# A two-layer hybrid-attention trunk: blocks 3 and 2, and 1 and 0, share one score step in three of its four branches

## What is computed

```python
h = split_cols(x @ w_in)
out_a = causal_dense_attention(qa, ka, va, key_valid, HEAD_DIM ** -0.5, decay)
out_b = mla_attention(h['b_cq'], h['b_ckv'], h['b_kr'], g_q, g_kv, w_uq, w_ukv, pos, key_valid)
out_c = dsa_sparse_attention(..., key_valid, rel_bias[:, :DSA_HEADS], top_k)
out_d = sliding_window_sink_attention(..., key_valid, rel_bias[:, DSA_HEADS:], sinks)
mixed = jnp.concatenate([
    out_a * jax.nn.silu(h['a_g']), out_b * jax.nn.silu(h['b_g']),
    out_c * jax.nn.silu(h['c_g']), out_d * jax.nn.silu(h['d_g'])], axis=-1)
return layer_norm(ALPHA * x + mixed @ w_out, ln_g, ln_b)
```

## Time and profile before

| | value |
|---|---|
| median of three runs | 2945.43 us (2944.47 to 2949.46) |
| the profiled execution's own time | 2943.56 us |
| span of the profiled execution | 2941.6 us |
| mean granted TensorE clock | 0.994 of full speed |
| TensorE busy | 2854.4 us, 97% of the span |
| VectorE, ScalarE, GpSimd busy | 55%, 36%, 22% |

### The profile page before, as it was taken

One profiled execution on the slowest core, in us unless ns is written; L12 is line 12 of the kernel. 1 busy time (PEld: TensorE's weight loads), 2 busy tenths in 40 slices (PEclk: granted clock), 3 DMA queues, 4 the chain that ended last, 5 costly groups with the idle time before them and its releaser, 6 DMA issues. The chain is left out here.

```text
span 2941.6 us, 39580 instructions
## 1 busy us (share of the span) xinstructions
PE 2854.4 (97%) x13638; PEld 1675.1 (57%) x13638; DVE 1621.2 (55%) x4361; ACT 1059.6 (36%) x3085; POOL 642.6 (22%) x1336
## 2 busy tenths in 40 slices
PE   7999999999999999999999999999999999999998
PEld 5446666555566666644544466665555666665443
DVE  5337888767776433322333388886767764323232
ACT  3334444343455345500012334443334544445000
POOL 1002333111122244500000022331112222444000
PEclk9999999999999999999999999999999999999999
DMA  6201111111110121042120011111011101201421
GB/s 225 66 8 47 44 44 33 38 33 45 37 32 19 33 99 33 26 149 79 58 91 31 10 45 44 44 33 45 28 43 37 33 17 33 106 28 30 155 86 43
DMA packets 90908, 156.88 MB, mean 53 GB/s; under 512 B 11296, under 2 KB 67248, under 8 KB 88920
## 3 DMA queue, kind: packets, MB, share of 16 engines
q1 hardware_dynamic: 90712, 154.36, 16.4%
HBM read 120.13 MB, written 32.08 MB: 52 GB/s over the span
## 5 line engine op out<-in xcount | busy, mean ns | idle before, releaser
L1160 PE MATMUL ps_s<-xT,w_ring 128*128 128x348 f32 (+4 forms) x3616 | 1122.4, 464 | 12.6 <-DVE gate L1617 5.0
L1160 PEld LDWEIGHTS ps_s<-xT,w_ring 128*128 128x128 f32 x3616 | 673.3, 191 | 396.4 <-issue 102.6
L1412 ACT ACTIVATE arena<-ps_t 16x32 f32<-16x32 f32 (+3 forms) x1048 | 367.2, 373 | 239.9 <-PE ps_t L1230 225.7
L1399 ACT ACTIVATE arena<-arena,small 128x1040 f32<-128x1040 f32 (+8 forms) x544 | 372.0, 684 | 132.4 <-DVE small L1679 131.6
L1442 DVE MAX8 small<-score 128x8 f32<-128x1040 f32 (+6 forms) x448 | 376.3, 840 | 10.5
L1444 DVE MATCH_REPLACE8 score<-small,score 128x1040 f32<-128x1040 f32 (+6 forms) x448 | 370.0, 826 | 0.0
L1230 PE MATMUL ps_t<-ident,arena 128*128 128x128 f32 (+1 forms) x2016 | 300.5, 278 | 13.0 <-ACT arena L1412 12.9
L1791 POOL TENSOR_SCALAR strips<-arena,small 128x16 f32<-128x16 f32 x384 | 107.1, 279 | 902.2 <-DVE small L1691 902.2
L1203 PE MATMUL ps_s<-feat 64*128 64x272 f32 (+12 forms) x1680 | 295.6, 454 | 3.3 <-ACT arena L1315 3.2
L1230 PEld LDWEIGHTS ps_t<-ident,arena 128*128 128x128 f32 (+1 forms) x2016 | 224.2, 140 | 116.6 <-issue 67.0
L1794 POOL TENSOR_SCALAR arena<-arena,small 128x1024 f32<-128x1024 f32 (+7 forms) x384 | 286.2, 745 | 0.0
(11 more groups left out here) (177 smaller groups left out, 2504.8 us busy)
## 6 DMA issues: line engine op xcount, KB each, us to landing
w_ring<-in_w_feat SPq DMA_DIRECT2D x78, 512.0 KB, 3.5
mixed<-mixg SPq DMA_DIRECT2D x128, 128.0 KB, 1.7
feat<-mixed SPq DMA_DIRECT2D x16, 1024.0 KB, 6.7
resid<-score SPq DMA_DIRECT2D x16, 512.0 KB, 3.2
score<-resid SPq DMA_DIRECT2D x16, 512.0 KB, 7.6
arena<-in_w_out SPq DMA_DIRECT2D x4, 1536.0 KB, 8.0
cT<-falls SPq DMA_DIRECT2D x8, 520.0 KB, 4.8
feat<-falls SPq DMA_DIRECT2D x8, 520.0 KB, 5.2
```

The costliest lines, as they stand in the source:

```text
L1160: mm = pe.matmul(ps_s[:, bank, 0:w], w_ring[:, wt % 2, k, :], xT[:, k, c0:c0 + w], start=(k == 0), stop=(k == KT - 1))
L1399: nc.scalar.activation(p, p, ACT.Exp, scale=-1.0, bias=nm[:, e:e + 1], accum_out=psums[0:M, st % 4, e:e + 1]).then_inc(S["exp_done"], 1)
L1412: a = nc.scalar.activation(dst, src, ACT.Copy)
```

## The change

It has these parts.

1. **Shared score steps.** In A, B and C the pair walks rounds of blocks, `[[8],[7],[6],[5],[4],[3,2],[1,0]]`; D keeps single blocks. One `qk` item holds the scores of both blocks of a round, and VectorE takes both maxima there. `rec` becomes a list: the reciprocals of blocks 3 and 2 stand behind the maxima of 1 and 0, those of 1 and 0 behind the maxima of the next pair's block 8. The `pv` of blocks 6 and 5 moves behind the scores of 1 and 0, that of 4 and 3 behind the next pair's first scores. In B, the scores of blocks 3 and 2 are no longer cut in two.
2. **C's fill.** G and the next pair's Q are written in half chunks (4 matmuls) at steps 0, 0, 1, 1, 2, 3, 4, 5, 6, 7, 7, 8; in p3 G's halves stand at 0, 0, 1, 1, 2, 3.
3. **B's fill.** From p1 on, the next pair's query products stand at steps 5, 6, 7 and no longer at 3, 4, 5.
4. **D's fill.** `LATENT_STEPS` gives TB and `ct` by a table: in p2 TB of 8 and 6 and `ct` of 5 at step 6, TB of 7 and `ct` of 8 at step 7, `ct` of 6 at step 8; in p3 `ct` of 7 moves from step 0 to step 1. The rotation's step 2 moves from step 6 to step 7.
5. **Top-256 search.** D runs 5 of its operations in steps 0 to 2 of p0 to p2, and in p3 4, 4, 4, 4, 3, 2, 2, 2, 3.
6. **Prologue.** Blocks are normalised in place; block 8 (the first) by VectorE, the others by ScalarE (one activation with scale and bias), for which GpSimd runs two more operations a block. A first activation loads ScalarE's table at the start, 20 transposes of nothing run on TensorE before the first block, and two small VectorE operations move behind the nine blocks.

```diff
+TOP_RATE = {..., "D": [5, 5, 5, 4, 4, 4, 4, 4, 4], "D3": [4, 4, 4, 4, 3, 2, 2, 2, 3], ...}
+LATENT_STEPS = [[([0], []), ([1], [0]), ([2], [1])], [([3], [2]), ([4], [3]), ([5], [4])],
+                [([8, 6], [5]), ([7], [8]), ([], [6])]]
...
+def rounds_of(br):
+    return [[i] for i in ORDER] if br == "D" else [[8], [7], [6], [5], [4], [3, 2], [1, 0]]
...
-        products = even(n, 2 if n >= 272 else 1)
+        products = even(n, 2 if i > 3 else 1)
...
+    def halves(self, l, what, **kw):
+        out, wt = [], self.open()
+        for c in (2, 1, 0) if what == "G" else range(3):
+            begun = {}
+            out.append(lambda c=c, begun=begun: begun.update(self.chunk(l, wt, what, c, k1=KT // 2, **kw)))
+            out.append(lambda begun=begun: self.add(**dict(begun, k0=KT // 2, k1=KT)))
+        return out
...
-                put(0, lambda: self.latent(l, NB - 2))
+                fill[1].insert(0, lambda: self.latent(l, NB - 2))
...
-                for idx, step in ((5, 0), (6, 1), (6, 2), (7, "dup")):
+                for idx, step in ((5, 0), (6, 1), (7, 2), (7, "dup")):
...
-                for idx, work in zip((3, 4, 5), self.q_latent(l, p + 1)):
+                for idx, work in zip((3, 4, 5) if p == 0 else (5, 6, 7), self.q_latent(l, p + 1)):
...
-            for idx, work in zip((3, 4, 5), self.tile(l, "Q", br="C", p=p + 1)):
+            rest = self.halves(l, "G", br=br, p=p) + self.halves(l, "Q", br="C", p=p + 1)
+            for idx, work in zip((0, 0, 1, 1, 2, 3, 4, 5, 6, 7, 7, 8), rest):
...
-        for idx, i in enumerate(ORDER):
+        for blocks in rounds_of(br):
+            steps = [self.step(l, br, p, i, hu) for i in blocks]
+            if steps:
+                self.add("qk", l=l, br=br, p=p, idx=steps[0]["idx"], hu=hu, steps=steps, ready=steps[0]["ready"])
+                self.normalise()
+                self.values()
+            self.pending += steps
+            for s in steps:
+                old = self.pending.pop(0) if len(self.pending) > LAG else None
+                if old and old["i"] == 0:
+                    self.values()
+                self.probabilities(old, 0)
+                self.add("exp", e=0, **s)
+                self.gated()
+                self.add("top", l=l, count=top_rate(br, p)[s["idx"]])
...
+            self.rec_next += steps
```

More of the change, by code:

```diff
@@ L414, in pair @@
         put = lambda idx, work: fill.setdefault(idx, []).append(work)
[L415 removed]
+        for idx, work in enumerate(self.tile(l, "G", br=br, p=p) if br != "C" else []):
             put(idx, work)
@@ L427, in pair @@
                     put(idx, work)
[L428 to L434, removed]
+                for idx, (blocks, turned) in zip((6, 7, 8), LATENT_STEPS[p]):
+                    for b in blocks:
+                        if b == NB - 1:
+                            put(idx, lambda: self.token_block(l, "TB", NB - 1, bank=self.free_bank()))
+                        else:
+                            put(idx, lambda b=b: self.token_block(l, "TB", b))
+                    for b in turned:
+                        put(idx, lambda b=b: self.latent(l, b))
                 if p == NP - 2:
@@ new lines, in pair, with step @@
+        if l == DEPTH - 1:
+            self.empty_step(l, br, p, early, fill.get(NB - 1, []))
+        return None
+    def step(self, l, br, p, i, hu):
+        st = self.take("st")
+        chunks, products = [], []
+        some = score_products(br, i)
+        for nth, ((c0, w), pieces) in enumerate(some):
+            banks = self.slot_for(len(some), nth, P_BANK)
+            last = self.n["chunk"] + len(pieces) - 1
+            waits = self.banks(banks, ("max_done", 2 * (last + 1)))
+            if O_BANK in banks:
+                waits = latest(waits + [("o_free", self.n["pv"])])
+            products.append(dict(c0=c0, w=w, banks=banks, pieces=len(pieces), waits=waits))
+            chunks += [dict(c0=a, w=b, banks=banks, at=a - c0, g=self.take("chunk"), full=2 * (last + 1))
+                       for a, b in pieces]
+        row, at = row_of(br, i)
+        owner = self.row_owner[row]
+        n = min(keys_of(i), 2 * BLK) if br == "D" else keys_of(i)
+        return dict(l=l, br=br, p=p, i=i, st=st, idx=NB - 1 - i, n=n, M=rows_of(i), chunks=chunks, products=products,
+                    row=row, at=ROW_AT[row] + at, ready=sorted(self.ready.items()) if i == NB - 1 else [],
+                    rwaits=latest([owner] if owner else []), a=(i + 1) // 2, hu=hu,
+                    ds=self.take("ds") if br == "D" else None, tri=self.take("tri") if br == "A" else None,
+                    nb=self.take("nb") if br == "C" else None)
@@ L1084, in _ @@
             pe.wait_ge(S["id_ld"], 16)
+            for _ in range(20):
+                pe.transpose(ps_t[:, 0, 0:BLK], ident[:], ident[:])
             for it in items:
@@ L1527, in _ @@
+                    if ln >= NB + 2:
+                        dve.wait_ge(x_st[r], 16 * len([n for n in range(ln - 1) if n % 2 == r]))
                         if it["xprev"]:
```

287 lines of the change are left out of this document (149 added, 138 removed).

## The result

The changed kernel takes 2956.83 us in the median of 7 runs (2954.79 to 2959.97), the kernel before 2945.43 us in as many. The ratio is 1.0040 with a 95% interval of 1.0030 to 1.0049: slower by 11.4 us. The forecast said no change, with 2946.0 us; the time lies in the stated range of 2925 to 2962 us, but outside the forecast's own 2938 to 2953. The profiled execution's span is 2952.9 us, 11.3 above that of before.

A forecast was written before the change was run, and what follows sets the result against it. The prediction took TensorE's fixed order as the bound. Its terms summed to +0.3 us on the profiled 2943.56 us; with the median's 1.87 us that is 2945.7, stated as 2946.0, no change, range 2925 to 2962 us.

The forecast's parts named there:

- Prologue, -5.5: Blocks before the index stage: no store wait before the norm, and shorter steps a block, -5.5 us.
- Shared scores, -2.4: A and C: two score sets side by side share part of a fixed cost, 24 meetings by 0.1, -2.4 us.
- A's tails, +6: A: block 3's late reciprocals make TensorE wait 1.3 us in p0 and p1, 0.2 in p2 and p3; +6 us.
- B's tails, +5: B: block 3's reciprocals move one step back, waits of 0.6 us a pair in the mean of eight, +5 us.
- D's fifth operation, +2.9: D's steps 0 to 2: the fifth search operation, with A's last reciprocals, costs +2.9 us for both layers.
- D's latents, +5.6: D: the 3.38 us wait stays, block 7's latent in p3 waits 4.3 us in place of 1.56; +5.6 us.
- End of D, -4.5: End of D: search operations and a rotation step leave, the 3.05 us wait falls to about 0.8; -4.5 us.
- The clock, -1.8: Half-speed stretches: +4 behind D's p3 wait, -3.4 behind the second layer's end of D, -2.4 in C; together -1.8 us.
- C's tails, -5: C's pair ends: half chunks let ScalarE's copies catch up, -1 for six pairs, +0.5 in each p3; -5 us.
- the 0.4 that the forecast set as its sign: C's p0 to p2: the changed profile would show no wait over 0.4 us.
- The second rival: A's and B's tails: each of sixteen pairs loses a whole VectorE operation more, +13 us, 2959 us; chance 0.18.
- The first rival: A's and B's tails are covered, their 6 and 5 us go, perhaps a clock dip too: 2931 us; chance 0.32.

The follow-up runs named there:

- best2_cold: best2 without the 20 transposes of nothing ahead of the prologue: 2919.31 us, ratio 0.9913 to the kernel before.
- ab_single: The changed kernel with A and B walking single blocks again, C keeping shared score steps: 2947.28 us, ratio 1.0006 to the kernel before.
- best1: The changed kernel with A, B single, B's query products and rotation's step 2 back, latent scaled before search, D's fifth search operation in steps 3 to 5: 2921.81 us.
- rot_back: The changed kernel with the rotation's step 2 back at step 6 of D's p3: 2951.28 us, ratio 1.0020 to the kernel before.
- c_single: The changed kernel with C walking single blocks again, half chunks kept: 2954.22 us, ratio 1.0032 to the kernel before.
- best2: best1 with C in single blocks too, so no shared score step is left: 2918.23 us, ratio 0.9914 to the kernel before.

## Why the prediction was right or wrong

*Prologue, -5.5: right.* -5.05, by the steps named; ScalarE's norm takes 1.24 us, inside the bounds. This execution has a half-speed stretch in its prologue; the six traces without one (run best2_cold, above) gain 6.2 to 6.5.

*Shared scores, -2.4: wrong in sign.* The step that failed is that two sets of scores side by side only share a start. They also leave two sets of transposes side by side, and these wait 0.4 us for a copy. In pairs without any wait for GpSimd (A's p2 and p3) the change is +0.13 to +0.25 us a pair, in C +0.1 to +0.25 against single blocks. The shared start itself came about as forecast: where the wait adds 0.4 us and the pair grows by 0.13 to 0.25, some 0.15 to 0.27 us a pair were saved.

*A's tails, +6: the mechanism right, the size too large.* VectorE is 1.8 us late where 1.5 was the estimate, and the wait in p1 is 1.14 where 1.3 was. But the second layer's waits are 0.75 and 0.90, and p2 and p3 have none: 3.8 us in all. A's pairs lost 5.6 us, near the 4.8 that the forecast makes with A's half of the shared scores, because the two misses cancel. That is luck.

*B's tails, +5: half of the mechanism.* B lost 9.0 us. Block 3's transposes wait 3.3 of them, in p0 and p1, as forecast and below the 5. The step that failed is that "only the 2.74 us `pv` moves with them": the forecast used this `pv` as cover for block 3 and didn't ask what it had covered before. That was block 4, whose 3.3 us of slack went, and which waits 4.1 us. B's moved query products have no term in the forecast at all; with single blocks they cost 1.8 us. Some 1.6 us of the 9.0 is a half-speed stretch at the start of B in the second layer, which went with the transfer's wait.

*D's fifth operation, +2.9: right* (1.42 and 1.60 us in p0, with A single, by ab_single against best1).

*D's latents, +5.6: right in place and size.* 3.39 us and 4.03 (4.16 in the second layer), where 3.38 and 4.3 were expected: the second wait grew by 2.5 and 2.6 us.

*End of D, -4.5: wrong.* "The wait falls to about 0.8 us" came true (0.82 and 0.97), but what is late next was not asked. Moving the rotation's step 2 one step on also moved the transfer of its result, which takes a median of 3.5 us from issue to landing in the kernel before (this row is of its DMA view: tile, issuer, count, size, time):

```profile
qr_two<-feat SPq DMA_DIRECT2D x2, 260.0 KB, 3.5
```

B's first scores wait 2.60 and 2.26 us for it. With the copy's wait that is 3.42 and 3.23 us, where 3.05 and 3.16 stood before: +0.4 instead of -4.5. This is the largest miss. Besides, D's new fill brings the waits of 0.65 and 0.64 us on ScalarE in p2 and p3, 2.6 us in both layers, for which the forecast has no term.

*The clock, -1.8: partly right.* The window behind the first layer's 3.38 us wait in the kernel before (columns as in rows 1):

```profile
721.00:726.00 5.00, 5.00 (x16) 3.07 (x16) 3.25 (x11) 2.59 (x11) 0.52 (x2) 0.50 0.52 197
```

Windows of the changed kernel, the first behind the same wait:

```profile
721.50:726.00 4.50, 4.50 (x23) 2.89 (x22) 3.25 (x11) 2.88 (x11) 0.53 (x2) 1.00 0.57 216
733.40:736.80 3.40, 3.24 (x8) 2.25 (x9) 0.10 (x1) 0.89 (x3) 0.00 (x0) 0.50 0.00 0
...
2204.50:2211.30 6.80, 4.46 (x10) 3.05 (x11) 2.22 (x6) 0.88 (x3) 0.00 (x0) 0.50 0.03 8
2252.30:2255.70 3.40, 3.40 (x16) 1.34 (x14) 0.00 (x0) 0.00 (x0) 0.00 (x0) 0.50 0.00 0
1590.10:1593.50 3.40, 3.40 (x8) 1.21 (x5) 2.94 (x14) 1.62 (x4) 0.00 (x0) 0.50 0.00 0
```

The lower level followed the 4 us wait in both layers, as said, and C's two stretches went. But it did not follow each of the two waits: behind the first layer's 3.39 us the granted clock reads 1.00, where the kernel before and the run rot_back, with the same wait, have 0.50. Behind the end of D in the second layer it did not go but moved behind the new wait, and one stretch came in the second layer's index stage. In the forecast's sum, -3.4 for a stretch with 6.25 busy us is a little much: half of them is 3.1.

*C's tails, -5: right in size, and the half chunks are the cause*, as c_single shows. Waits of 0.41 and 0.52 us stay in p1 and p2, just above the 0.4 that the forecast set as its sign.

The parts missed by +0.45 (prologue), +0.8 (A with its share of the scores' -2.4), +4.0 (B), +3.9 (D with its clock) and +1.9 us (C with its clock): 11 us between the +0.3 of the sum and the +11.3 of the spans. D's +3.9 hides a larger miss. Up to B's first scores TensorE waits 10.4 us longer than before in the two layers, where the forecast's terms without the clock make 4.0, and less half speed in D (13.7 us of it in place of 20.5) took some of that back. The second rival's time (2959) was near, but not its mechanism: GpSimd's 13.3 us are close to the 11 that the forecast itself gave A's and B's tails, and 7.1 of them stand where it put them, before block 3. The first rival fell.

## What to carry to other kernels

Putting two like steps together on the engine that bounds the kernel also moves what fed it: ask which result now has one step less to arrive, what the work that moved had covered until then, and what stood between two uses of the same buffer. When work on a side engine is moved later to free the path, follow its output too, through its transfer, to whoever reads it first. A scaling that the bound engine waits for belongs ahead of filler on its engine: that order alone was worth 15 us here, more than the change's whole effect.

## What the runs showed of the hardware

Equal waits did not always bring the same clock. In best1 a wait of 0.77 us in B's p1 was followed by half speed, in best2 the same wait with the same work was not:

```profile
876.09 0.33 PE L1297 MATMUL ps_t<-ident,arena 128*128 128x128 f32 x1 [0.77 <-ACT arena L1490]
...
877.20 3.46 PE L1314 MATMUL ps_o<-arena 128*64 128x256 f32 x20 [0.38 <-ACT arena L1490]
```

```profile
874.52 0.33 PE L1297 MATMUL ps_t<-ident,arena 128*128 128x128 f32 x1 [0.77 <-ACT arena L1490]
...
875.63 1.88 PE L1314 MATMUL ps_o<-arena 128*64 128x256 f32 x20 [0.37 <-ACT arena L1490]
```

The same 20 matmuls took 3.46 and 1.88 us, and this p1 58.01 and 56.43. Most pairs with the same work have lengths that repeat to 0.02 us between kernels; one into which such a stretch of 3.4 us falls is about 1.6 us longer. The Trainium skill, "TensorE: Matmul & The Clock Gate", Part 1, says that one kernel shows different numbers of slow matmuls at its start from run to run. The prologues here agree: the second block's 8 transposes take 1.92 us in best1 and 1.06 in best2, whose instructions are the same up to there.

```profile
13.44 1.92 PE L1166 MATMUL ps_t<-ident,arena 128*128 128x128 f32 x8 [2.33 <-ACT xT L1369]
```

```profile
13.54 1.06 PE L1166 MATMUL ps_t<-ident,arena 128*128 128x128 f32 x8 [1.65 <-ACT xT L1369]
```

At the start of the kernel before, 16 matmuls took 4.05 us and the same 16 at 22.08 took 2.13 us, half and full speed by their lengths:

```profile
15.58 4.05 PE L1130 MATMUL ps_s<-arena,xT 128*128 128x144 f32 x16
...
22.08 2.13 PE L1130 MATMUL ps_s<-arena,xT 128*128 128x144 f32 x16
```

The granted clock in the window around the first of them (columns as in rows 1) still reads 1.00:

```profile
13.85:17.30 3.45, 3.45 (x16) 3.45 (x17) 1.07 (x3) 1.50 (x4) 0.79 (x2) 1.00 1.02 395
```

Two other rows bear this out: the second block's 8 transposes took 1.94 us here with 1.00 in the column, and 1.92 us in best1 with 0.50. So at the start of these executions the lengths of equal matmuls tell the clock, not that column.
